# First dense chunks between the transposes of x, another order of the first loads, norm weights as rows, no copy of x to the output

## The reference

```python
for l in range(DEPTH):
    h = rms_norm(x, norm_g[l])          # x * rsqrt(mean(x*x) + eps) * norm_g
    p = h @ w_in[l]                     # split by columns into the branches and gates
    # A) stick-breaking attention, 4 heads x 128
    # B) latent attention, 8 heads, low-rank q and kv, rotary key
    # C) RWKV-7 time mixing, 8 heads x 64, on p_rw mixed with its row before
    merged = (g_sb * (y_sb @ w_br_sb[l]) + g_mla * (y_mla @ w_br_mla[l])
              + g_rw * (y_rw @ w_br_rw[l]))
    x = x + merged @ w_out[l]
return x
```

## Time and profile before

| | |
|---|---|
| Time of three runs, median (lowest to highest) | 1819.05 us (1818.07 to 1819.42) |
| The profiled execution, its own time | 1821.68 us |
| Its span | 1819.9 us |
| PE busy | 1778.6 us (98%) |
| PE weight load | 1498.6 us (82%) |
| DVE busy | 1074.2 us (59%) |
| ACT busy | 880.7 us (48%) |
| POOL busy | 138.9 us (8%) |
| Mean granted clock of PE | 0.997 |
| DMA | 335.19 MB, mean 184 GB/s |

### The profile page before, as it was taken

How to read it: one execution, slowest core, us unless ns; L and a number is a source line. 1 busy time by engine, 2 the same in 40 slices (tenths; PEclk the granted TensorE clock), 3 DMA queues, 4 the chain that set the end, 5 groups by cost and what they waited for, 6 DMA issues and landing times.

```text
span 1819.9 us, 22316 instructions
## 1 busy us (share of the span) xinstructions
PE 1778.6 (98%) x8912; PEld 1498.6 (82%) x8912; DVE 1074.2 (59%) x1388; ACT 880.7 (48%) x1234; POOL 138.9 (8%) x159
## 2 busy tenths in 40 slices
PE   6899999999999999999999999999999999999998
PEld 5678888889888888788888788888888888887887
DVE  3568454554866645686556774645557656467753
ACT  4444444334454666455544444434344555765532
POOL 1010111211000000100000010201100000001000
PEclk9999999999999999999999999999999999999999
DMA  7865555445565554785677655546456555558754
GB/s 235 237 192 177 173 159 165 149 143 170 174 187 154 165 152 153 258 281 181 208 231 236 188 164 154 170 139 183 135 168 193 160 159 159 150 174 309 238 188 155
DMA packets 178943, 335.19 MB, mean 184 GB/s; under 512 B 22556, under 2 KB 35258, under 8 KB 178168
## 3 DMA queue, kind: packets, MB, share of 16 engines
q1 hardware_dynamic: 169816, 297.67, 53.7%
q0 software_dynamic: 9024, 36.10, 5.6%
HBM read 313.56 MB, written 18.87 MB: 183 GB/s over the span
## 4 chain that ended last, share of the span: by engine, by line
PE 87%; DMA 4%; DVE 3%; ACT 3%; issue 1%; SPq 1%; ACTq 0%; DVEq 0%
PE D L578 73%; PE B L578 11%; DMA ring<-in_w_in 2%; DMA ring<-in_w_br_rw 2%; ACT arena L887 1%; DVE w_lo L1195 1%; DVE arena L1195 1%; ACT L887 1%; ACT w_hi L887 1%; PE B L632 0%; DVE xy L1195 0%; PE B L648 0%; PE B L867 0%; DMA xy<-in_x 0%; DVE gev L1233 0%
## 5 line engine op out<-in xcount | busy, mean ns | idle before, releaser
L1195 DVE TENSOR_TENSOR w_lo<-ring,w_hi 128x1024 fp32r<-128x1024 f32 (+3 forms) x560 | 661.7, 1195 | 457.0 <-ACT w_hi L887 448.5
L887 ACT ACTIVATE w_hi<-ring 128x1024 fp32r<-128x1024 f32 (+3 forms) x560 | 572.9, 1037 | 388.1 <-PE D L578 279.8
L578 PE MATMUL D<-w_hi,ht_hi 128*128 128x512 f32 (+2 forms) x1728 | 692.0, 400 | 16.4 <-DVE w_lo L1195 13.3
L578 PE MATMUL D<-w_hi,ht_lo 128*128 128x512 f32 (+2 forms) x1728 | 668.4, 387 | 0.0
L578 PE MATMUL D<-w_lo,ht_hi 128*128 128x512 f32 (+2 forms) x1728 | 666.8, 386 | 0.0
L578 PEld LDWEIGHTS D<-w_hi,ht_hi 128*128 128x128 f32 x1728 | 326.7, 189 | 80.4 <-DVE w_lo L1195 15.9
L578 PEld LDWEIGHTS D<-w_hi,ht_lo 128*128 128x128 f32 x1728 | 325.8, 189 | 67.3
L578 PEld LDWEIGHTS D<-w_lo,ht_hi 128*128 128x128 f32 x1728 | 327.0, 189 | 57.2 <-issue 0.5
L578 PEld LDWEIGHTS B<-arena 128*128 128x128 f32 (+3 forms) x1568 | 205.2, 190 | 24.6 <-issue 7.6
L578 PE MATMUL B<-arena 128*128 128x128 f32 (+5 forms) x1568 | 220.3, 293 | 1.4 <-DVE arena L1369 1.1
L887 ACT ACTIVATE arena<-B 128x512 f32<-128x512 f32 (+4 forms) x168 | 81.0, 491 | 286.7 <-PE B L578 229.3
(11 more groups left out here) (135 smaller groups left out, 1276.7 us busy)
## 6 DMA issues: line engine op xcount, KB each, us to landing
ring<-in_w_in SPq DMA_DIRECT2D x368, 512.0 KB, 3.9
ring<-in_w_out SPq DMA_DIRECT2D x64, 512.0 KB, 4.8
ring<-in_w_br_mla SPq DMA_DIRECT2D x32, 512.0 KB, 4.7
gate_spill<-gev POOLq DMA_DIRECT2D x24, 512.0 KB, 4.2
arena<-gate_spill POOLq DMA_DIRECT2D x24, 512.0 KB, 4.9
ring<-in_mla_w_ukv SPq DMA_DIRECT2D x16, 512.0 KB, 4.1
ring<-in_w_br_rw SPq DMA_DIRECT2D x16, 512.0 KB, 6.4
ring<-in_w_br_sb SPq DMA_DIRECT2D x16, 512.0 KB, 5.3
```

The lines of the kernel that those rows point to most:

```text
L578: return nc.tensor.matmul(o, a, b, start=start, stop=stop, skip_group_check=True)
L887: return nc.scalar.activation(o, i, fn, **kw)
L1195: return v.tensor_tensor(o, a, b, op)
```

## The change

The diff, with what only declares names left out:

```diff
@@ tiles
         GR = take(128)
+        NG16 = GR[0:KD, :]
@@ SyncE
-            for j in range(4):
+            def first_x(j):
                 c = slice(j * 512, (j + 1) * 512)
-                if j == 0:
-                    sp.dma_start(con[:, 0:P], consts[:, 0:P]).then_inc(id_in, 16)
                 sp.dma_start(xy[:, :, c], x[0, :, c].rearrange("(h p) d -> p h d", p=P)).then_inc(x_moved[j], 16)
-                if j == 0:
-                    with nc.allow_non_contiguous_dma("gains as columns"):
-                        sp.dma_start(ng, columns(norm_g[0])).then_inc(first_gain, 16)
-                if j < LEAD:
-                    for d0, m, src in pieces(0, j, 0):
-                        sp.dma_start(ring[:, j, :, d0:d0 + m], src).then_inc(first_w[j], 16)
+
+            def first_chunk(n):
+                for d0, m, src in pieces(0, n, 0):
+                    sp.dma_start(ring[:, n, :, d0:d0 + m], src).then_inc(first_w[n], 16)
+
+            sp.dma_start(con[:, 0:P], consts[:, 0:P]).then_inc(id_in, 16)
+            first_x(0)
+            sp.dma_start(NG16, norm_g[0].rearrange("(k p) -> k p", p=P)).then_inc(gain_rows, 16)
+            first_x(1)
+            first_chunk(0)
+            first_chunk(1)
+            first_x(2)
+            first_chunk(2)
+            first_x(3)
@@
-                    if l == 0 and n == RING:
-
-                        sp.wait_ge(first_lo, LEAD)
-                        sp.wait_ge(first_sq, 4)
-                        sp.wait_ge(first_xl, 8)
+                    if l == 0 and RING <= n < RING + LEAD:
+                        sp.wait_ge(first_lo, n - RING + 1)
@@ GpSimd
             pool.wait_ge(first_sq, 4)
-
-            pool.wait_ge(split_lo, 2)
-            pool.dma_start(con[:, P:K_END], consts[:, P:K_END]).then_inc(con_in, 16)
-            pool.wait_ge(split_lo, 6)
-            pool.dma_start(out[0], x[0]).then_inc(x_copy, 16)
@@
                 shift(PW, WK[:, :, 64:192], wk_shift[l])
+                if l == 0:
+                    pool.wait_ge(split_lo, END["wk"] + 2)
+                    pool.dma_start(con[:, P:K_END], consts[:, P:K_END]).then_inc(con_in, 16)
@@
-                        pool.wait_ge(x_copy, 16)
                         pool.wait_ge(x_settled[l], 4)
-                        pool.dma_start(xy[:], out[0].rearrange("(h p) d -> p h d", p=P)).then_inc(x_in[l], 16)
+                        pool.dma_start(xy[:], (out if l else x)[0].rearrange("(h p) d -> p h d", p=P)
+                                       ).then_inc(x_in[l], 16)
@@ TensorE, dense_to
-                        if l and gi == 0:
+                        if gi == 0:
                             pe.wait_ge(xt_dve[l - 1], c + 1)
+                            if l == 0 and c < LEAD:
+                                pe.wait_ge(first_lo, c + 1)
@@ TensorE, start
-            for j in range(4):
-                pe.wait_ge(x_moved[j], 16)
-                if j >= 2:
-                    pe.wait_ge(first_xl, 2 * j - 2)
-                transposes((2 * j, 2 * j + 1), j * 512, first_pe)
-            pe.wait_ge(first_xl, 8)
-            pe.wait_ge(first_lo, LEAD)
             for l in range(DEPTH):
                 at[0] = beats[0] = 0
-                if l:
+                if l == 0:
+                    for j in range(4):
+                        pe.wait_ge(x_moved[j], 16)
+                        if j >= 2:
+                            pe.wait_ge(first_xl, 2 * j - 2)
+                        transposes((2 * j, 2 * j + 1), j * 512, first_pe)
+                        if j == 0:
+                            pe.wait_ge(gain_rows, 16)
+                            mm(D[3][:, 0:KD], NG16, ident[0:KD, 0:KD], True, True).then_inc(gain_columns, 1)
+                        else:
+                            dense_to(2 * j)
+                else:
@@ ScalarE, start
-            act.wait_ge(first_gain, 16)
-            for j in range(4):
-                act.wait_ge(x_moved[j], 16)
-                columns_hi(j, first_pe, first_xh)
-                squares(j, first_sq)
-                if j < LEAD:
-                    act.wait_ge(first_w[j], 32)
-                    f(wh[:, j, :, 0:256], ring[:, j, :, 0:256]).then_inc(first_hi, 1)
+            act.wait_ge(gain_columns, 1)
+            f(ng, D[3][:, 0:KD]).then_inc(first_gain, 1)
+            act.wait_ge(first_gain, 1)
@@ (first_split(n): that split of chunk n; first_squares(j): squares of piece j)
+                if l == 0:
+                    columns_hi(0, first_pe, first_xh)
+                    first_split(0)
+                    first_split(1)
+                    columns_hi(1, first_pe, first_xh)
+                    first_split(2)
+                    dense_to(1)
+                    columns_hi(2, first_pe, first_xh)
+                    dense_to(3)
+                    columns_hi(3, first_pe, first_xh)
+                    dense_to(4)
+                    first_squares(0)
+                    first_squares(1)
+                    dense_to(5)
+                    first_squares(2)
+                    dense_to(6)
+                    first_squares(3)
+                    dense_to(7)
+                else:
...
-                dense_to(BRIDGE + 2)
+                    dense_to(BRIDGE + 2)
                 act.wait_ge(x_sum[l - 1], 1)
@@ VectorE, start
-            dve.wait_ge(first_gain, 16)
-            for j in range(4):
-                columns_lo(j, first_xh, first_xl)
-                if j < LEAD:
-                    dve.wait_ge(first_hi, j + 1)
-                    tt(wl[:, j, :, 0:256], ring[:, j, :, 0:256], wh[:, j, :, 0:256].bitcast(F32), ALU.subtract
-                       ).then_inc(first_lo, 1)
-            sum_squares(first_sq, first_sum)
+            dve.wait_ge(first_gain, 1)
...
+                if l == 0:
+                    columns_lo(0, first_xh, first_xl)
+                    first_split(0)
+                    first_split(1)
+                    columns_lo(1, first_xh, first_xl)
+                    first_split(2)
+                    dense_to(1)
+                    columns_lo(2, first_xh, first_xl)
+                    dense_to(3)
+                    columns_lo(3, first_xh, first_xl)
+                    dense_to(6)
+                    sum_squares(first_sq, first_sum)
```

More of the change, by code:

```diff
@@ L354, in program @@
         x_moved = [ctx.enter_context(nc.semaphore(f"x_moved{j}")) for j in range(4)]
-        x_copy = ctx.enter_context(nc.semaphore("x_to_out"))
         first_w = [ctx.enter_context(nc.semaphore(f"first_weights{c}")) for c in range(LEAD)]
         first_gain, first_hi, first_lo = (one("first_" + n) for n in ("gains", "weights_hi", "weights_lo"))
+        gain_rows, gain_columns = one("gain_rows_in"), one("gain_columns")
         first_pe, first_xh, first_xl, first_sq, first_sum = (s[-1] for s in (xt_pe, xt_act, xt_dve, x_sq, x_sum))
@@ L1090, in _, with first_split, first_squares @@
             act.preload_act_table_set("natural_log_exp_and_others")
-            act.wait_ge(first_gain, 16)
-            for j in range(4):
+            act.wait_ge(gain_columns, 1)
+            f(ng, D[3][:, 0:KD]).then_inc(first_gain, 1)
+            act.wait_ge(first_gain, 1)
+            def first_split(n):
+                act.wait_ge(first_w[n], 32)
+                f(wh[:, n, :, 0:256], ring[:, n, :, 0:256]).then_inc(first_hi, 1)
+            def first_squares(j):
                 act.wait_ge(x_moved[j], 16)
-                columns_hi(j, first_pe, first_xh)
                 squares(j, first_sq)
-                if j < LEAD:
-                    act.wait_ge(first_w[j], 32)
-                    f(wh[:, j, :, 0:256], ring[:, j, :, 0:256]).then_inc(first_hi, 1)
             for l in range(DEPTH):
                 at[0] = group[0] = beats[0] = 0
-                if l:
+                if l == 0:
[17 more added lines that the diff above has]
+                else:
                     dense_to(BRIDGE)
@@ L1432, in sum_squares, with first_split @@
                 v.tensor_reduce(ss, sums.rearrange("p (h j) -> p h j", h=2), axis=X, op=ALU.add).then_inc(done, 1)
-            dve.wait_ge(first_gain, 16)
-            for j in range(4):
-                columns_lo(j, first_xh, first_xl)
-                if j < LEAD:
-                    dve.wait_ge(first_hi, j + 1)
-                    tt(wl[:, j, :, 0:256], ring[:, j, :, 0:256], wh[:, j, :, 0:256].bitcast(F32), ALU.subtract
-                       ).then_inc(first_lo, 1)
-            sum_squares(first_sq, first_sum)
+            def first_split(n):
+                dve.wait_ge(first_hi, n + 1)
+                tt(wl[:, n, :, 0:256], ring[:, n, :, 0:256], wh[:, n, :, 0:256].bitcast(F32), ALU.subtract
+                   ).then_inc(first_lo, 1)
+            dve.wait_ge(first_gain, 1)
             for l in range(DEPTH):
```

## The result

| | before | after |
|---|---|---|
| first comparison, median (lowest to highest) | 1819.18 us (1818.07 to 1819.42) | 1806.03 us (1803.65 to 1811.34) |
| ratio | | 0.9933, 95% interval 0.9917 to 0.9949 |
| profiled execution, its span | 1819.9 us | 1809.6 us (time 1811.34 us) |
| DMA | 335.19 MB | 333.10 MB |

The forecast was 1806.0 us for the median, and 1808.6 us for a profiled execution. In two further comparisons the changed kernel had medians of 1809.18 and 1805.63 us, with ratios 0.9939 (0.9926 to 0.9953) and 0.9920 (0.9908 to 0.9933). So each step is read from the place in the trace where it acts, and the median comes second.

What follows compares the result with a forecast made beforehand. PE, busy 98% of the span, was taken as the bound, with idleness to win only before chunk 12. 16.0 - 1.0 - 1.5 - 0.4 = 13.1 us off 1819.05 gave 1806.0 us, range 1802.8 to 1811.8.

Steps and rivals of the forecast that it cites:

- What bounds it, and where the gain lies: Whole kernel: PE busy 98% of the span; all the change can win lies before chunk 12's start at 56.44 us.
- the allowances: Taken off the 16.0 us gain at chunk 12: 1.0 for its load, 1.5 for the constants, 0.4 for the clock.
- Gains as rows: Start: the 3.32 us issue behind the column load goes; x piece 1 lands at 7 to 8, columns_hi starts at 8.1.
- Chunks 0 to 8: Start: chunk 0 at 11.3 instead of 20.81, waits of 1.4 us before chunks 7 and 8, chunk 8 at 29.5.
- What is late next: Ring loads from chunk 12 on: 1 us lost for chunk 12's later load, 1.5 for the constants beside chunks 13 to 16.
- the sharing rule: DMA engines alternate between queues with work, so POOL loads slow SP's ring; by it alone the ring is 3.5 us later.
- All of it lies before chunk 12.: Whole gain of 13.1 us falls before chunk 12; wrong if the time moves by anything after group rv.
- The allowance for DMA: Ring loads around chunks 12 to 16: 1.0 us for chunk 12's load and 1.5 for the constants, 2.5 together.
- The low clock: Rival, start through group wk: PE stays at the low clock, chunk 12 at 46.5, gain 7.4, 1811.6 us; chance 0.12.
- held by DMA: Rival, ring loads: one late chunk costs 8.2 us instead of 2.5, gain 7.4, 1811.6 us; chance 0.16.
- The start was faster: Opposed rival, start no faster: chunk 8 held at 34.2, only the stalls go, gain 8.9, 1810.2 us; chance 0.06.
- Slower: Rival, chunks 12 to 20: constants collide with the ring, three late chunks, 8.6 us slower, 1827.7 us; chance 0.04.

Runs made afterwards that it cites:

- no_copy_only: Kernel before without the copy of x to the output, x read from the input at the end of layer 0: 1813.56 us, ratio 0.9964.
- pool_only: Kernel before with only POOL's part of the change (constants late, no copy of x, x read from the input): 1813.06 us, ratio 0.9959.
- gain_columns: Changed kernel with the norm weights loaded as columns again, without the small matmul and ACT's copy: 1806.21 us, ratio 0.9929.
- squares_early: Changed kernel with ACT's squares moved into the gaps in which it waits: 1807.87 us, ratio 0.9931.
- copy_back: Changed kernel with the copy of x to the output again, x read back from the output: 1809.86 us, ratio 0.9950.
- squares_con_early: Changed kernel with ACT's squares in its gaps and the constants issued where they were before: 1811.85 us, ratio 0.9948.
- joined: Changed kernel with squares in ACT's gaps, early constants, transposes of wk columns half a chunk later, x reload after the sixth gate load: 1801.39 us, ratio 0.9897.

## Why the prediction came out right, point by point

*What bounds it, and where the gain lies.* Right for the gain. Chunk 12 at 40.81 was predicted at 40.4 before the allowances; no_copy_only and pool_only put 10.0 us on the copy (beside the constants and the row), 1.2 on the constants and 4.6 on the new order.

*Gains as rows.* `columns_hi` at 8.20 (predicted 8.1). That the held-up issue "goes" is true and worth nothing: gain_columns. Piece 1 came at 8.86, not at 7 to 8.

*Chunks 0 to 8.* Chunk 0 at 11.55 (11.3), the low pace until 15.95, 4.4 us after its start (4.0), transposes hot in 1.03, waits for the squares 1.26 and 1.10 (1.4 each), chunk 8 at 29.80 (29.5). squares_early shows that the cause is the one named. What I did not see is that taking this cost away would gain nothing. The 0.4 us allowed for a later rise of the clock came as forecast.

*What is late next.* This step failed, though the number came out right. I took 1.0 us for chunk 12's load and 1.5 for the constants, among chunks 12 to 16. PE waited for no chunk there. What came instead was a longer wait at the transposes after chunk 15, by 0.3 to 1.0 us in the three profiled executions (1.33 to 1.96 against 1.00), and whether the constants make it is not shown. The terms are mis-sized: 2.5 allowed, at most 1.0 measured.

*The trace agrees with the sharing rule* of the Trainium skill, "DMA: Bandwidth & Descriptors", Queues, rings and completion order, in kind: ring loads are late where a POOL load is in flight (ACT's 4.48 us in squares_early, 6.14 in copy_back). The 3.5 us worked out from it holds for no place of the changed kernel. The prediction's sentence beside it names chunks 9 and 10 as late; the earlier trace rows have the waits before 9 and 11.

*"All of it lies before chunk 12."* Wrong, by my own test for it. 15.6 - 1.0 would have been 1804.4 us. The rest was lost in layer 1 in some executions: the merge's wait and the falls of the clock. For the profiled execution, where they all came together, the forecast of 1808.6 missed: it took 1811.34. The allowance for DMA that was not needed stood in for them, so the closeness of 1806.0 to 1806.03 is luck in good part; 1809.18 and 1805.63 show how much.

*Rivals.* The low clock didn't stay through `wk`. No chunk was held by DMA in the changed kernel; squares_con_early and joined show that this rival was only 2.4 us of PE's time away. The start was faster. Slower did not come near.

## What to carry to other kernels

A transfer that nobody waits for can still set the time: the copy of 2 MB, read by nobody for 700 us, cost 10 us beside the constants and a 768 KB row, and 2 to 4 us by itself in the new order, by the loads it made late. Where PE is fed by a ring of loads that just keep up, as here, a gain upstream is kept only if the ring has slack at the next load that is put beside it; look for that load before moving work forward. And check single waits in several executions before a median is explained: here the waits of 2.5 us at the two merges, far behind the chunks that the change moves, were worth 4 us together.

## What was not expected of the hardware

The clock fell after waits that are far shorter than the 6.34 us of the earlier trace rows, and not always. At the merge near 1645 us, in 14 profiled executions, it fell in the six whose wait was 2.7 us or more (2.7, 3.1, 3.1, 3.3, 3.4, 4.4) and in none of the eight with 2.5 or less. But at the merge of layer 0, near 751 us, it fell only in squares_con_early, after 2.17 us, and not after 2.54 in two others. Near 658 us, with the same 1.8 us wait for `w_lo` each time, it fell in eight of them (658 to 673 us) and not in six. So the length of one wait does not decide alone. The Trainium skill, "TensorE: Matmul & The Clock Gate", HAM oscillation, puts such falls down to idle gaps; the trace agrees in kind for the merge of layer 1, where the longer waits brought the fall, and the place near 658 us shows that it can fall after a wait of 1.8 us too. What decides there stays open.
